# A fused mixer and MoE layer on one core: input rows and router rows transposed by VectorE through DRAM scratch, and the low parts of the mixer's weights kept in DRAM

## The chip, the cores and the metric

The kernel runs on one core of a Trainium2 chip. The metric is the device time of one execution in microseconds (us). Five engines run their own queues in order and meet at semaphores: TensorE (PE; its weight loads are listed as PEld), VectorE (DVE), ScalarE (ACT), GpSimd (POOL) and SyncE (SP), which here only issues DMAs. ScalarE and GpSimd issue DMAs too, and such an instruction, like a wait, holds up whatever stands behind it in its engine's queue.

## The reference

2048 tokens of 1024 channels, all in float32, one layer:

```python
h    = layer_norm(x, ln_in_g, ln_in_b)
proj = h @ w_in                      # (2048, 2048): pool v | gate B | gate C | conv u
pool = (trailing mean over 2/4/8/16 tokens - v) @ pool_w * pool_scale       # 4 groups of 128
conv = gate_b * (causal_depthwise_conv3(gate_c * u) + conv_b)               # 512 channels
h    = layer_norm(ALPHA * h + concat(pool, conv) @ w_out, ln1_g, ln1_b)     # "h1" below
ffn  = MoE(h)    # router h @ w_router (16 experts), softmax, best group of 4, its top 2, silu(x@w1)*(x@w3) @ w2
out  = layer_norm(ALPHA * h + ffn, ln2_g, ln2_b)
```

## The kernel before

**High and low parts.** A float32 product is made of three matmuls in a faster format. Each operand is split into a high part, a copy rounded to that format (ScalarE, `split_hi`), and a low part, the operand less its high part (VectorE, `split_lo`). `three` multiplies high x high, high x low and low x high into one bank of PSUM.

**Chunks and units.** The mixer works through the tokens in 4 chunks of 512 (`NCH`), each of 4 tiles of 128 rows (`TPC`). A chunk has 12 units of weights (`CU`), each 128 x 2048 numbers: units 0 to 7 are columns of `w_in`, two units for each of four groups `g`, and units 8 to 11 are `w_out`. A unit is 48 matmuls. In units 0 to 7 its two halves of 24 are called sections: sections 0 and 1 in the even unit (gate C and u), 2 and 3 in the odd unit (pool v and gate B); section n goes to bank `acc[n]`. Units live in a ring of four slots, `ring_hi` and `ring_lo`. SyncE loads a unit into one of two `stage` buffers, ScalarE makes its high part three units ahead of its use, VectorE its low part. The same 12 units are loaded and split anew in each chunk.

**One unit on the helpers.** All order is written out by hand. For each unit `j` each engine's `chunk` does its share, in this order in its queue. ScalarE: `unit_ahead` (the high part of unit j + 3), then what is listed below for h1, then for an even `j` the high part of the finished convolution and the copy of section 1 to `zext`, for an odd `j` the high part of the pooled product, a convolution tap, the copy of section 2 to `vext`, and the high part of the pooled rows. VectorE: the low part of unit j + 3, then for an even `j` `z_rows` (which reads `zext`) and `conv_lo`, for an odd `j` `pool_mix_lo`, `pool_rows` (which reads `vext`), `conv_rows` and `pooled_split`; after these the normalising `ln_h1` in units 0 to 3, and at the end of an odd unit `gate_rows`.

**The rows of h and h1.** The matmuls need h with channels on the partitions. For chunk c + 1, VectorE normalises the tiles of h in `hrow` during chunk c (`ln_h`), TensorE transposes them 128 x 128 at a time into the banks `tp` (`tr_tile`, before unit 8 and after units 8 to 10), ScalarE and VectorE take high and low parts from there (`tr_hi`, `tr_lo`). GpSimd stores h to DRAM for the residual sum. After a chunk, VectorE adds the residual, and in units 0 to 3 of the next chunk `ln_h1` makes h1 of the four tiles in `hres`; GpSimd stores each (`h1_norm`). In units 2 to 5 TensorE transposes h1 (`h1_tile`), ScalarE copies it to `h1t` (`h1t_copy`, units 3 to 6), TensorE multiplies it by the router's weights (`route_tile`, after units 3 to 6). In units 4 to 7 ScalarE scales h1 by ALPHA and stores it (`alpha_h1`), and in units 5 to 8 it issues the load of the h rows that the residual sum of this chunk needs (`res_load`). The last chunk's h1 goes another way (`h1_last`), and then the experts follow.

## Time and profile before

| | us |
|---|---|
| Median of 3 runs | 1347.22 (1345.38 to 1347.94) |
| The profiled execution | 1347.38 |
| Its span, first to last instruction | 1345.5 |
| TensorE busy | 1310.9 (97%) |
| VectorE busy | 969.2 (72%) |
| ScalarE busy | 510.8 (38%) |
| GpSimd busy | 515.4 (38%) |

The mixer takes the first 600 us, the experts the rest. The page gives the span, the busy time of each engine with its share, and the chain of work that ended last. Views of the trace go closer: windows give one line for each stretch (bounds, length, then busy time and number of instructions of PE, PEld, DVE, ACT and POOL, the granted clock of TensorE as a share of full speed, the busy share of the DMA engines, and GB/s); a timeline gives an engine's instructions by start and duration with the idle time before them and its releaser in brackets. L1194 is line 1194 of the kernel.

### The profile page before, as it was taken

To read this page: it belongs to the slowest core of one execution; us is meant where nothing else is said; L and a number is where in the kernel's file an instruction comes from. 1 tells how busy PE (TensorE), PEld (TensorE's weight loads), DVE (VectorE), ACT (ScalarE), POOL (GpSimd) and SP (SyncE) were. 2 spreads that over 40 slices of the span, in tenths; PEclk is the share of its full clock that TensorE was granted. 3 is DMA by queue.
4 is the path that set the end of the run, shared out by engine and by line. 5 is a ranking of instruction groups with operands and counts; after the bars stand their busy time and mean duration, and the time that the engine had idled before them with its cause. 6 is when DMAs were issued, how large, how long until landed. Compare 5 with 4: busy or idle time off the path is not lost.

```text
span 1345.5 us, 20470 instructions
## 1 busy us (share of the span) xinstructions
PE 1310.9 (97%) x6382; PEld 1096.3 (81%) x6383; DVE 969.2 (72%) x1358; ACT 510.8 (38%) x568; POOL 515.4 (38%) x543
## 2 busy tenths in 40 slices
PE   5999999999999999998999999999999999999995
PEld 5888888888888888887888888888888888888884
DVE  7758577687759786698777885775775677777574
ACT  3423234322343234324444554433442454443351
POOL 2001110111101010022566665656555556665655
PEclk9999999999999999999999999999999999999998
DMA  9625434564455344544877774564555545766421
GB/s 271 177 87 164 147 108 169 163 192 117 156 178 167 111 141 146 208 184 167 307 263 266 264 264 145 190 231 140 183 196 186 184 169 210 237 235 233 152 70 64
DMA packets 156523, 243.59 MB, mean 181 GB/s; under 512 B 18944, under 2 KB 84992, under 8 KB 156480
## 3 DMA queue, kind: packets, MB, share of 16 engines
q1 hardware_dynamic: 118624, 154.15, 35.0%
q0 software_dynamic: 28928, 71.74, 15.1%
q10 hardware_dynamic: 8928, 17.13, 3.7%
q8 instruction: 26, 0.43, 0.1%
q14 instruction: 17, 0.14, 0.0%
HBM read 211.97 MB, written 64.62 MB: 206 GB/s over the span
## 4 chain that ended last, share of the span: by engine, by line
PE 94%; DVE 2%; issue 1%; DMA 1%; POOL 1%; DVEq 0%; ACT 0%; SPq 0%; POOLq 0%
PE acc L520 28%; PE acc L522 28%; PE acc L521 28%; PE tp L560 4%; PE logits L599 2%; PE aux L830 1%; DMA b_in<-in_ln_in_b 1%; PE logits L645 0%; DVE ring_lo L1650 0%; DMA xg<-h_scratch,gat_now 0%; DVE ring_lo L1239 0%; PE aux L522 0%; PE aux L521 0%; PE aux L520 0%; PE aux L670 0%
## 5 line engine op out<-in xcount | busy, mean ns | idle before, releaser
L520 PE MATMUL acc<-ring_hi 128*128 128x512 f32 (+1 forms) x800 | 309.1, 386 | 1.8 <-DVE ring_lo L1239 1.6
L522 PE MATMUL acc<-ring_hi,ring_lo 128*128 128x512 f32 (+1 forms) x800 | 305.7, 382 | 0.0
L521 PE MATMUL acc<-ring_lo,ring_hi 128*128 128x512 f32 (+1 forms) x800 | 305.4, 382 | 0.0
L520 PE MATMUL acc<-ring_hi,xt_hi 128*128 128x512 f32 x648 | 256.4, 396 | 2.4 <-issue 2.2
L522 PE MATMUL acc<-ring_hi,xt_lo 128*128 128x512 f32 x648 | 252.8, 390 | 0.0
L521 PE MATMUL acc<-ring_lo,xt_hi 128*128 128x512 f32 x648 | 252.5, 390 | 0.0
L1803 POOL TENSOR_TENSOR small<-small 128x1 f32<-128x1 f32 x31 | 47.4, 1528 | 360.8 <-DVE small L1208 360.8
L520 PEld LDWEIGHTS acc<-ring_hi 128*128 128x128 f32 x800 | 151.4, 189 | 29.9 <-DVE ring_lo L1239 2.4
L522 PEld LDWEIGHTS acc<-ring_hi,ring_lo 128*128 128x128 f32 x800 | 151.3, 189 | 29.1
L521 PEld LDWEIGHTS acc<-ring_lo,ring_hi 128*128 128x128 f32 x800 | 151.5, 189 | 27.6
L1650 DVE TENSOR_TENSOR ring_lo<-stage_x,ring_hi 128x2048 fp32r<-128x2048 f32 x60 | 161.2, 2727 | 0.2
L921 ACT CAST ring_hi<-stage_x 128x2048 fp32r<-128x2048 f32 x64 | 119.4, 1915 | 77.9 <-PE acc L522 77.3
L520 PEld LDWEIGHTS acc<-ring_hi,xt_hi 128*128 128x128 f32 x648 | 121.9, 188 | 27.2 <-issue 2.8
L522 PEld LDWEIGHTS acc<-ring_hi,xt_lo 128*128 128x128 f32 x648 | 121.6, 188 | 25.6
L521 PEld LDWEIGHTS acc<-ring_lo,xt_hi 128*128 128x128 f32 x648 | 121.8, 188 | 24.0
L916 ACT CAST ring_hi<-stage 128x2048 fp32r<-128x2048 f32 x47 | 89.7, 1909 | 101.5 <-PE acc L522 97.3
L520 PE MATMUL acc<-ring_hi,ht_hi 128*128 128x512 f32 x312 | 125.1, 401 | 0.9 <-DVE ht_lo L1586 0.9
L1194 DVE TENSOR_TENSOR ring_lo<-stage,ring_hi 128x2048 fp32r<-128x2048 f32 x47 | 107.6, 2288 | 20.6 <-ACT ring_hi L916 20.5
L522 PE MATMUL acc<-ring_hi,ht_lo 128*128 128x512 f32 x312 | 121.9, 391 | 0.0
L521 PE MATMUL acc<-ring_lo,ht_hi 128*128 128x512 f32 x312 | 121.6, 390 | 0.0
L1662 DVE TENSOR_TENSOR rrow<-srow,acc 128x512 f32<-128x512 f32 x78 | 49.9, 680 | 95.7 <-PE acc L522 91.8
L1956 POOL DMA_INDIRECT xg<-h_scratch,gat_now x39 | 46.6, 1194 | 146.5 <-PE tp L560 125.9
(277 smaller groups left out, 1922.7 us busy)
## 6 DMA issues: line engine op xcount, KB each, us to landing
stage_x<-in_exp_w SPq DMA_DIRECT2D x64, 1024.0 KB, 6.9
stage<-in_w_in SPq DMA_DIRECT2D x64, 512.0 KB, 5.4
stage<-in_exp_w SPq DMA_DIRECT2D x32, 1024.0 KB, 7.1
stage<-in_w_out SPq DMA_DIRECT2D x32, 512.0 KB, 5.1
h_scratch<-hres POOLq DMA_DIRECT2D x16, 512.0 KB, 3.0
sum_scratch<-hres ACTq DMA_DIRECT2D x16, 512.0 KB, 2.9
hrow<-in_x POOLq DMA_DIRECT2D x12, 512.0 KB, 4.7
h_scratch<-hrow POOLq DMA_DIRECT2D x12, 512.0 KB, 3.0
```

What stands on the lines that cost most here:

```text
L520: nc.tensor.matmul(dst, w_hi, x_hi, start=start, stop=False)
L521: nc.tensor.matmul(dst, w_hi, x_lo, start=False, stop=False)
L522: return nc.tensor.matmul(dst, w_lo, x_hi, start=False, stop=stop)
L560: mm = nc.tensor.transpose(banks[b][:, q, :], rows[:, k * P:(k + 1) * P], ident[:])
L599: mm = nc.tensor.matmul(dst, h1t[:, k, :], wr[:, k, :], start=(k == 0), stop=(k == KT - 1))
L916: nc.scalar.copy(ring_hi[:, slot:slot + 1, :], staged(slot_in)).then_inc(s_hi, 1)
L921: nc.scalar.copy(ring_hi[:, j:j + 1, :], staged(j)).then_inc(s_ehi[j // 2], 1)
L1194: V.tensor_tensor(lo, staged(slot_in), hi.bitcast(F32), ALU.subtract).then_inc(s_lo, 1)
L1650: V.tensor_tensor(ring_lo[:, j:j + 1, :], staged(j), ring_hi[:, j:j + 1, :].bitcast(F32), ALU.subtract).then_inc(s_elo[w], 1)
L1662: ins = V.tensor_tensor(rrow[:, cols], srow[:, cols], acc[2 + n][:], ALU.add)
L1803: G.tensor_tensor(rstd[:], vareps[:], half[:], ALU.pow).then_inc(s_rstd, 1)
L1956: G.indirect_dma_start(xg[:], None, h1_dram, bass.IndirectOffsetOnAxis(ap=index[:, 0:1], axis=0), bounds_check=SEQ - 1, oob_is_err=False). ...
```

## The change

The changed kernel does three things otherwise.

**VectorE transposes.** VectorE's transpose works within blocks of 32 x 32. So that these blocks are enough, a tile is first rearranged in quarters through DRAM: for h, GpSimd stores the normalised tile in that arrangement (`h0_rows`) and loads it back (`h_back`), VectorE transposes it into the banks `tp` (`h_turn`); for h1, ScalarE loads the stored h1 rows back into `hres` with four DMAs of 32 partitions (`h1_back`), and VectorE transposes them straight to `h1t` (`h1_turn`). The channels come out in another order (`(p k)` in place of `(k p)`), so `w_in` and `w_router` are loaded in that order, and the transposes that stay on TensorE (chunk 0 and the last h1) read with a step of eight numbers. `tr_tile` for chunks 1 to 3, `h1_tile` and `h1t_copy` are gone.

**Places.** `alpha_h1` moves from units 4 to 7 to units 1 to 4, `h1_back` stands in units 2 to 5, `res_load` in units 4 to 7 with a wait for `h1_turn`; `h1_turn` stands at the end of VectorE's units 3 to 6; `route_tile` stands in the middle of TensorE's units 4 to 7. `ln_h` of tile 1 moves from unit 7 to unit 6.

**Low parts.** Only the 12 low parts of chunk 0 are computed. SyncE stores them to DRAM (`keep_lo`), and for the other 36 units it loads them back (`back_lo`), each 1 MB, two units behind the load of the unit itself. TensorE waits for the high part and for that load (`unit_split`).

```diff
+            def keep_lo(u):
+                sp.dma_start(lo_dram[u], ring_lo[:, u % RING1, :].bitcast(F32)).then_inc(s_kept[u % RING1], 16)
+            def back_lo(u):
+                if u < CU + RING1:
+                    sp.wait_ge(s_kept[u % RING1], 16 * (CU // RING1))
+                sp.dma_start(ring_lo[:, u % RING1, :].bitcast(F32), lo_dram[u % CU]).then_inc(s_back[u % RING1], 16)
...
+            for u in range(CU, MU):
+                if u < CU + 2:
...
+                else:
+                    sp.wait_ge(s_hi, u - 1)
+                    load_mixer(u % CU)
+                    back_lo(u - 2)
...
+            def unit_split(u):
+                if u < CU:
+                    pe.wait_ge(s_lo, u + 1)
+                else:
+                    pe.wait_ge(s_hi, u + 1)
+                    pe.wait_ge(s_back[u % RING1], 16 * ((u - CU) // RING1 + 1))
...
             def route_tile(c, t):
-                pe.wait_ge(s_h1tc, (c * TPC + t + 1) * 2)
+                pe.wait_ge(s_h1turn, c * TPC + t + 1)
...
                         section(slot, which, sct).then_inc(s_sec[sct], 1)
+                        if not first and which == 0 and j >= 4:
+                            route_tile(c - 1, j - 4)
...
-                    if not first:
-                        if 3 <= j < 7:
-                            route_tile(c - 1, j - 3)
-                        if 2 <= j < 6:
-                            h1_tile(c - 1, j - 2)
...
             def alpha_h1(c, t):
                 act.wait_ge(s_h1out[t], c * 16 + 16)
-                act.wait_ge(s_h1t, (c * TPC + t + 1) * 2)
+                if c == NCH - 1:
+                    act.wait_ge(s_h1t, (t + 1) * 2)
...
+            def h1_back(c, t):
+                act.wait_ge(s_ahout[t], c * 16 + 16)
+                rows = h1_dram[(c * TPC + t) * P:(c * TPC + t + 1) * P, 0:D].rearrange("(r b) (a f) -> a r b f", r=SUB, a=QUARTERS)
+                for a in range(QUARTERS):
+                    dst = hres[a * SUB:(a + 1) * SUB, t, :].rearrange("r (b f) -> r b f", b=QUARTERS)
+                    act.dma_start(dst, rows[a]).then_inc(s_h1q[t], 16)
...
-                    if not first and 3 <= j < 7:
-                        h1t_copy(c - 1, j - 3)
+                    if not first and 1 <= j < 5:
+                        alpha_h1(c - 1, j - 1)
+                    if not first and 2 <= j < 6:
+                        h1_back(c - 1, j - 2)
                     if not first and 4 <= j < 8:
-                        alpha_h1(c - 1, j - 4)
-                    if not first and 5 <= j < 9:
-                        res_load(c, j - 5)
+                        res_load(c, j - 4)
...
             def unit_ahead(c, j, last):
                 ja = j + RING1 - 1
-                if ja >= CU and last:
+                if c * CU + ja >= CU:
                     return
...
+            def h_turn(c, t):
+                dve.wait_ge(s_xq[t % 2], ((c - 1) * 2 + t // 2 + 1) * 16)
+                dve.wait_ge(s_trlo, (c * TPC + t) * 2)
+                by_k = hrow[:, t % 2, :].rearrange("p (b c k) -> p k b c", b=QUARTERS, c=SUB)
+                for h in range(2):
+                    V.transpose(tp[h][:].rearrange("p q (r b) -> p q b r", r=SUB), by_k[:, 4 * h:4 * h + 4]).then_inc(s_tr, 1)
+            def h1_turn(c, t):
+                dve.wait_ge(s_h1q[t], (c + 1) * 16 * QUARTERS)
+                dve.wait_ge(s_log, c * TPC + t)
+                if c >= 1 and t == 0:
+                    dve.wait_ge(s_lst, c)
+                V.transpose(h1t[:].rearrange("p k (r b) -> p k b r", r=SUB),
+                            hres[:, t, :].rearrange("p (b c k) -> p k b c", b=QUARTERS, c=SUB)).then_inc(s_h1turn, 1)
...
+                    if not first and 3 <= j < 7:
+                        h1_turn(c - 1, j - 3)
                     if not last:
-                        if j in (5, 7):
-                            ln_h(c + 1, (j - 5) // 2, nth())
+                        if j in (5, 6):
+                            ln_h(c + 1, j - 5, nth())
+                        if j == 7:
+                            h_turn(c + 1, 0)
```

On ScalarE, in units 1 and 2 of chunk 2, the queue of before reads (L1023 is the convolution tap, L916 the high part of a coming unit, L1028 the copy to `vext`, L955 the high part of a convolution, L1016 the copy to `zext`):

```order
L1023 ACTIVATE cacc<-zext,cb,cw 128x512 [waits mix_lo,z_ready]
L1028 COPY vext<-acc 128x512 [waits pooled,sec_v]
L1030 CAST ring_hi<-sum_a 128x512 [waits pooled]
L916 CAST ring_hi<-stage 128x2048 [waits stage1_in,sec_b]
L955 CAST ring_hi<-cacc 128x512 [waits conv_rows]
L1016 COPY zext<-acc 128x512 [waits sec_u,conv_rows]
```

and that of the changed kernel, where the same steps have lines L1061, L951, L1066, L990 and L1054:

```order
L1001 ACTIVATE hres<-hres 128x1024 [waits h1_out0]
L1003 DMA sum_scratch<-hres 128x1024 [waits alpha_h1]
L1061 ACTIVATE cacc<-zext,cb,cw 128x512 [waits mix_lo,z_ready]
L1066 COPY vext<-acc 128x512 [waits pooled,sec_v]
L1068 CAST ring_hi<-sum_a 128x512 [waits pooled]
L951 CAST ring_hi<-stage 128x2048 [waits stage1_in,sec_b]
L1001 ACTIVATE hres<-hres 128x1024 [waits h1_out1]
L1003 DMA sum_scratch<-hres 128x1024 [waits alpha_h1]
L1011 DMA hres<-h_scratch 32x4x256 [waits alpha_h1_out0]
L1011 DMA hres<-h_scratch 32x4x256 x3
L990 CAST ring_hi<-cacc 128x512 [waits conv_rows]
L1054 COPY zext<-acc 128x512 [waits sec_u,conv_rows]
```

The scaling (L1001), its store (L1003) and the loads of h1 rows (L1011) stand ahead of the tap, of the copy to `vext` and of the copy to `zext`; before, they came from unit 4 on.

On VectorE, at the end of unit 3 and the start of unit 4 of chunk 2, before (L1287 is `pooled_split`, L1216 the last step of normalising the fourth tile of h1, L1292 `gate_rows`, L1194 a unit's low part, L1246 the start of `z_rows`):

```order
L1287 TENSOR_TENSOR ring_lo<-sum_a,ring_hi 128x512 [waits pooled_hi_done,dve_chain]
L1204 BN_STATS small<-hres 128x6 [waits res_taken]
L1205 BN_STATS small<-hres 128x6
L1207 BN_AGGR small<-small 128x2 [waits dve_chain]
L1208 TENSOR_SCALAR small<-small 128x1 [waits dve_chain]
L1212 SCALAR_TENSOR_TENSOR hres<-hres,small,g_52 128x1024
L1216 SCALAR_TENSOR_TENSOR hres<-hres,small,b_53 128x1024 [waits rstd_ready,dve_chain]
L1292 TENSOR_TENSOR cacc<-cacc,acc 128x512 [waits sec_b]
L1194 TENSOR_TENSOR ring_lo<-stage,ring_hi 128x2048 [waits unit_hi]
L1246 COPY zext<-zhist 128x2 [waits sec_u_free,sec_c]
```

and in the changed kernel:

```order
L1344 TENSOR_TENSOR ring_lo<-sum_a,ring_hi 128x512 [waits pooled_hi_done,dve_chain]
L1244 BN_STATS small<-hres 128x6 [waits res_taken]
L1245 BN_STATS small<-hres 128x6
L1247 BN_AGGR small<-small 128x2 [waits dve_chain]
L1248 TENSOR_SCALAR small<-small 128x1 [waits dve_chain]
L1252 SCALAR_TENSOR_TENSOR hres<-hres,small,g_52 128x1024
L1256 SCALAR_TENSOR_TENSOR hres<-hres,small,b_53 128x1024 [waits rstd_ready,dve_chain]
L1349 TENSOR_TENSOR cacc<-cacc,acc 128x512 [waits sec_b]
L1288 STREAM_TRANSPOSE h1t<-hres 128x8x4x32 [waits lists_done,logits_done,h1_quarters_in0]
L1303 COPY zext<-zhist 128x2 [waits sec_u_free,sec_c]
```

The low part is gone, and the transpose of the first tile of h1 (L1288) stands behind the normalising of the fourth.

On TensorE, the router product of the first tile of h1 in chunk 2 (L599 before) stood between units 3 and 4, beside the transposes of the second tile (L560):

```order
L521 MATMUL acc<-ring_lo,ring_hi 128x512
L522 MATMUL acc<-ring_hi,ring_lo 128x512
L599 MATMUL logits<-wr,h1t 128x16 [waits h1_t_copied]
L599 MATMUL logits<-wr,h1t 128x16 x7
L560 MATMUL tp<-ident,hres 128x128 [waits h1_t_copied,h1_rows]
L560 MATMUL tp<-ident,hres 128x128 x7
L520 MATMUL acc<-ring_hi 128x512 [waits sec_c_free,unit_lo]
L521 MATMUL acc<-ring_lo,ring_hi 128x512
```

In the changed kernel (L639) it stands between the two sections of unit 4 and waits for VectorE's transpose:

```order
L556 MATMUL acc<-ring_hi 128x512
L557 MATMUL acc<-ring_lo,ring_hi 128x512
L558 MATMUL acc<-ring_hi,ring_lo 128x512
L639 MATMUL logits<-wr,h1t 128x16 [waits h1_quarters_turned]
L639 MATMUL logits<-wr,h1t 128x16 x7
L556 MATMUL acc<-ring_hi 128x512 [waits sec_u_free]
L557 MATMUL acc<-ring_lo,ring_hi 128x512
```

## Rows read from the trace of the kernel before

**Rows 1.** The page: the span, and busy time of the engines

```profile
span 1345.5 us, 20470 instructions
...
PE 1310.9 (97%) x6382; PEld 1096.3 (81%) x6383; DVE 969.2 (72%) x1358; ACT 510.8 (38%) x568; POOL 515.4 (38%) x543
```

**Rows 2.** Windows, chunks 1 and 2: busy us, clock, DMA share, GB/s

```profile
160.00:309.00 149.00, 149.00 (x728) 125.18 (x727) 107.22 (x167) 50.34 (x58) 19.74 (x21) 1.00 0.50 156
309.00:457.00 148.00, 148.00 (x728) 124.16 (x727) 111.82 (x194) 48.49 (x58) 18.67 (x19) 1.00 0.48 150
```

**Rows 3.** Chain that ended last, chunk 2: start us, us, what

```profile
318.77 0.89 PE aux L670 x8
...
342.15 0.87 PE tp L560 x8
...
353.95 1.69 PE logits L599 x16
355.64 0.92 PE tp L560 x8
...
408.63 0.88 PE tp L560 x8
```

**Rows 4.** Timeline of VectorE, end of chunk 1 and chunk 2: start, us, instruction

```profile
291.81 1.28 DVE L1216 SCALAR_TENSOR_TENSOR hrow<-hrow,small,b_in 128x1024 f32<-128x1024 f32 x1 [0.54 <-POOL small L1803]
...
323.97 1.28 DVE L1216 SCALAR_TENSOR_TENSOR hres<-hres,small,b 128x1024 f32<-128x1024 f32 x1 [0.54 <-POOL small L1803]
...
327.98 0.17 DVE L1259 COPY vext<-vhist 128x16 f32<-128x16 f32 x1
...
336.94 0.68 DVE L1292 TENSOR_TENSOR cacc<-cacc,acc 128x512 f32<-128x512 f32 x1
...
351.32 0.16 DVE L1259 COPY vext<-vhist 128x16 f32<-128x16 f32 x1
...
355.65 0.69 DVE L1287 TENSOR_TENSOR ring_lo<-sum_a,ring_hi 128x512 fp32r<-128x512 f32 x1
...
361.01 0.68 DVE L1292 TENSOR_TENSOR cacc<-cacc,acc 128x512 f32<-128x512 f32 x1
361.61 2.28 DVE L1194 TENSOR_TENSOR ring_lo<-stage,ring_hi 128x2048 fp32r<-128x2048 f32 x1
```

**Rows 5.** Timeline of ScalarE, chunk 2, the same columns

```profile
325.18 0.59 ACT L1028 COPY vext<-acc 128x512 f32<-128x512 f32 x1 [3.21 <-PE acc L522]
...
371.33 1.08 ACT L973 ACTIVATE hres<-hres 128x1024 f32<-128x1024 f32 x1
372.44 0.33 ACTq L975 DMA_DIRECT2D sum_scratch<-hres  x1
372.86 0.39 ACTq L981 DMA_DIRECT2D hres<-h_scratch  x1
```

**Rows 6.** Timeline of GpSimd, the store of chunk 1's first h1 rows

```profile
325.85 0.58 POOL L1830 DMA_DIRECT2D h_scratch<-hres  x1 [1.99 <-DVE hres L1216]
```

**Rows 7.** Stores of h1 rows (line L1830), issue to landing

```profile
DMA to landing us min/median/max: 2.9/3.0/4.0
```

**Rows 8.** Stores of scaled h1 rows (line L975), issue to landing

```profile
DMA to landing us min/median/max: 2.6/3.0/5.5
```

**Rows 9.** DMA issues of one line: KB each, median us to landing

```profile
hres<-h_scratch ACTq DMA_DIRECT2D x12, 512.0 KB, 4.8
```

**Rows 10.** Timeline of VectorE, two reductions of the same 256 elements

```profile
422.54 0.42 DVE L1323 TENSOR_REDUCE lost<-wins 128x64 f32<-128x256 f32 x1
422.88 0.60 DVE L1323 TENSOR_REDUCE won<-wins 128x64 f32<-128x256 f32 x1
```

**Rows 11.** Timeline of TensorE at the start, matmuls with 256 columns

```profile
17.66 0.58 PE L520 MATMUL acc<-ring_hi 128*128 128x256 f32 x1 [1.63 <-DVE ring_lo L1239]
...
21.67 0.34 PE L520 MATMUL acc<-ring_hi 128*128 128x256 f32 x1
...
24.35 0.28 PE L521 MATMUL acc<-ring_lo,ring_hi 128*128 128x256 f32 x1
```

More of the change, by code:

```diff
@@ L64 @@
 ROW = D + NE
+SUB = 32
+QUARTERS = P // SUB
 ALIGN = 128
@@ L97, in build, with h0_tile, h0_rows @@
     h0_dram = nc.dram_tensor("h0_scratch", (SEQ, D), F32).ap()
+    def h0_tile(tile):
+        return h0_dram[tile * P:(tile + 1) * P, :]
+    def h0_rows(tile):
+        return h0_tile(tile).rearrange("(a r) (b f) -> (r b) a f", r=SUB, b=QUARTERS)
     h1_dram = nc.dram_tensor("h1_scratch", (SEQ, ROW), F32).ap()
@@ L352, in build @@
         s_lo = sem("unit_lo")
+        s_kept = [sem(f"slot{i}_lo_stored") for i in range(RING1)]
+        s_back = [sem(f"slot{i}_lo_loaded") for i in range(RING1)]
         s_used = sem("unit_used")
@@ L384, in build @@
         s_h1t = sem("h1_transposed")
+        s_h1q = [sem(f"h1_quarters_in{t}") for t in range(TPC)]
+        s_h1turn = sem("h1_quarters_turned")
         s_h1tc = sem("h1_t_copied")
@@ L486, in _ @@
                     x_first(j + 2)
-            for c in range(1, NCH):
-                for j in range(CU):
-                    sp.wait_ge(s_lo, c * CU + j - 1)
-                    load_mixer(j)
+                else:
+                    keep_lo(j - 2)
+            for u in range(CU, MU):
+                if u < CU + 2:
+                    sp.wait_ge(s_lo, u - 1)
+                    load_mixer(u % CU)
+                    keep_lo(u - 2)
+                else:
+                    sp.wait_ge(s_hi, u - 1)
+                    load_mixer(u % CU)
+                    back_lo(u - 2)
+            for u in range(MU, MU + 2):
+                sp.wait_ge(s_hi, u - 1)
+                back_lo(u - 2)
             def load_expert(ex, j):
@@ L553, in first_units, with transpose_h @@
                             elif bank == 2:
-                                tr_tile(0, 2)
+                                tr_tile(2)
+            def transpose_h(rows, banks):
+                by_k = rows.rearrange("p (c k) -> p k c", k=KT)
+                for b in range(2):
+                    for q in range(4):
+                        mm = nc.tensor.transpose(banks[b][:, q, :], by_k[:, 4 * b + q, :], ident[:])
+                    mm.then_inc(s_tr, 1)
             def transpose_tile(rows, sem_out, banks=tp):
@@ L713, in chunk @@
                     if j == 8:
-                        if not last:
-                            tr_tile(c + 1, 0)
                         pe.wait_ge(s_mix, (c * NG + 3) * 2)
@@ L735, in chunk @@
                         list_tiles(c - 1)
-                    if not last and j < CU - 1:
-                        tr_tile(c + 1, j - 7)
                 if last:
-                    pe.wait_ge(s_lo, c * CU + CU)
+                    unit_split(c * CU + CU - 2)
+                    unit_split(c * CU + CU - 1)
                     for t in range(TPC):
@@ L959, in route_exp @@
                 nc.scalar.activation(rt[c].prob[:], rt[c].shift[:], ACT.Exp).then_inc(s_exd, 1)
-            def h1t_copy(c, t):
-                if c >= 1 and t == 0:
-                    act.wait_ge(s_lst, c)
-                for b in range(2):
-                    act.wait_ge(s_h1t, (c * TPC + t) * 2 + b + 1)
-                    nc.scalar.copy(h1t[:, 4 * b:4 * b + 4, :], tp[b][:]).then_inc(s_h1tc, 1)
             def alpha_h1(c, t):
                 act.wait_ge(s_h1out[t], c * 16 + 16)
-                act.wait_ge(s_h1t, (c * TPC + t + 1) * 2)
+                if c == NCH - 1:
+                    act.wait_ge(s_h1t, (t + 1) * 2)
                 nc.scalar.mul(hres[:, t, :], hres[:, t, :], ALPHA).then_inc(s_ah, 1)
@@ L1504, in chunk @@
                         if j == 11:
+                            residual(c, 1, 0)
+                            h_turn(c + 1, 3)
+                            residual(c, 1, 1)
                             tr_lo(c + 1, 3)
-                            for t in range(TPC):
-                                residual(c, 1, t)
+                            residual(c, 1, 2)
+                            residual(c, 1, 3)
                     else:
```

63 lines of the change are left out of this document (37 added, 26 removed).

## Prediction

> **What bounds the kernel now.** I read the page first: TensorE is busy for 1310.9 of a span of 1345.5 us, VectorE for 969.2 [rows 1]. A busy TensorE could still be waiting on something, so I took the stretches by chunk next: in chunks 1 and 2 TensorE is busy for every microsecond at the full granted clock, while VectorE has 107 to 112 us of work in some 149 and the DMA engines are half used [rows 2]. So in the mixer every instruction taken off TensorE is worth its whole time, as long as nothing starts to make TensorE wait. The chain that ended last shows what such an instruction costs [rows 3]: eight transposes of one tile take 0.87 to 0.92 us, and a unit of 48 matmuls takes 353.95 - (342.15 + 0.87) = 10.93 us, so half a unit (one section) 5.47. After the matmuls I read the three helpers in chunk 2, because the change rewires them: VectorE [rows 4], ScalarE [rows 5] and GpSimd's stores [rows 6 to 8].
>
> **The change, part by part.**
>
> *Transposes off TensorE.* 12 tiles of h and 12 of h1, eight transposes each. The rows give 0.88 for a tile of h, 0.87 for the first tile of h1 in a chunk, and 0.92 for the other three, which follow a router product [rows 3]: 12 x 0.87 + 12 x 0.91 = **-21.3 us**, all of it on the chain.
>
> *VectorE's load.* 36 subtractions of 2048 elements go, 2.28 us each [rows 4]: -82 us. 24 block transposes of 512 elements and 12 of 1024 come. No row of before has one. The nearest is a pair of reductions over the same 256 elements: read in order 0.42 us, read with a step of 16 bytes 0.60 us [rows 10]. That is 0.7 ns more for each element. VectorE does 2048 elements in 2.28 us and 512 in 0.69 us [rows 4], so 1.04 ns an element and a fixed 0.16; with the step 0.16 + 512 x 1.74 ns = 1.05 us, and 1.94 us for 1024. Bounds: 0.69 and 1.22 us if the step costs nothing, and 3 us and 6 us if each element takes three such steps. I take 1.05 and 1.94, together 48 us: VectorE's load falls by 34 us. The Trainium skill, "Vector Engine (DVE) Microarchitecture Reference", on the reshape front-end, says that the transposing array sustains one element per cycle per lane; by that the two would be 0.69 and 1.22 us. The sum would fall by 3 x 0.7 = 2 us, since only one h1 transpose per chunk lies on the path below.
>
> *The low parts.* They are read back right after the high part of the same unit is made, three units (33 us) before TensorE wants them, and 1 MB more on the queue is hidden by that. Traffic of a chunk grows from 150 GB/s x 148 us = 22 MB [rows 2] by 12.6 MB of low parts and 4.2 MB of rows read back, so the share of the DMA engines goes from 0.48 to some 0.8. Cost nothing by themselves; without that cover a unit would wait for its load.
>
> *The round trip of h.* Tile 3 of h is the last: before, its normalising ended at 293.1 [rows 4] and the next chunk began at 318.77 - 10.93 = 307.8 [rows 3], 14.7 us. After, there are 0.6 + 3.0 us of store, some 4.8 of load (what the residual rows take [rows 9]), 2.1 of transposes, and 1.9 for its high and low parts: 12.4 us. It fits with 1 to 2 us to spare. Nothing charged.
>
> *The wait that the change adds.* This is the term that decides. The scaling of h1 on ScalarE (`alpha_h1`) moves from units 4 to 7 to units 1 to 4. It waits for the store of the normalised row, and VectorE normalises tile t only in unit t. Behind the scaling, ScalarE's queue holds the copy of the section that VectorE's next step reads (`vext`, `zext`). So each tile now goes VectorE, store, ScalarE, VectorE, with nothing beside it, and TensorE waits at the end, at the router product of tile 0, which now stands in the middle of unit 4. I walk chunk 2 on the clock of the trace of before:
> - Tile 0: rows ready at 325.25 [rows 4], store issued 325.85 [rows 6], landed 3.0 later [rows 7] at 328.9. ScalarE scales and issues in 1.11 + 0.42 = 1.53 us [rows 5], 330.4. Then a convolution tap of some 0.75 and the `vext` copy of 0.59 [rows 5]: 331.7. Before, that copy was done at 325.8 [rows 5].
> - VectorE from the pooling of unit 1 to the end of normalising tile 1 needs 336.94 - 327.98 = 8.96 us [rows 4]: 340.7. Store issued 341.3, landed 344.3, scaled and issued 345.9, four `h1_back` issues of 0.42 [rows 5]: 347.5, two more ScalarE steps of 512 elements (high part, `zext` copy), 1.1: 348.6.
> - VectorE: 1.5 us for z and a low part (two steps of 512 elements and small ones), 4.75 to normalise tile 2 (361.01 - 355.65 less 0.61 [rows 4]): 354.9. Store landed 358.5, scaled 360.0, issues 361.7, pooled high part, tap, `vext`: 363.6.
> - VectorE, pooling of unit 3 to the end of tile 3: 361.01 - 351.32 = 9.69 us [rows 4]: 373.3. Gate 0.6, `h1_turn` 1.94: 375.8.
> - TensorE: unit 3 starts at 342.15 as before but without the transposes, ends at 353.1, first section of unit 4 at 358.5. It waits for tile 0's transposed rows until 375.8: **17.3 us**.
>
> Nothing later in the chunk waits by the same walk: the transposes of tiles 1 to 3 come a unit apart and VectorE is ahead again by unit 7. Three chunks: **+52 us**.
>
> *What the loaded queues add.* Three stores of each chunk lie in that walk, nine in all, and each comes while up to 2 MB for a coming unit is under way. Measured stores land in 2.6 to 5.5 us [rows 7, 8]. I charge 0.5 us over the median: **+4.5** (bounds 0 and 9 x 2 = 18). The Trainium skill, "DMA: Bandwidth & Descriptors", section "Issuing engines are not separate DMA queues", says that the queues of all issuing engines run on the same 16 DMA engines and interleave, which speaks for the upper bound, by which the sum would be 14 us more.
>
> *TensorE's clock.* The only long idle time of before is at the start, and after it matmuls of 256 columns came every (21.67 - 17.66) / 19 = 0.211 us, later every (24.35 - 21.67) / 22 = 0.122 [rows 11]: the rates of 1.2 and 2.4 GHz. The 19 slow ones cost 19 x 0.089 = 1.7 us. Three waits of 17 us: **+5.2**. The Trainium skill, "TensorE: Matmul & The Clock Gate", section "Why this matters for your kernels", warns of idle gaps between bursts of matmuls for this reason; by it the term stands, without it the sum is 5 us less.
>
> *Strided transposes that stay.* 64 transposes on TensorE (chunk 0 and the last h1) now read with a step of 32 bytes. No row shows it. If the step costs TensorE what it costs VectorE, two thirds more on 128 reads of 0.42 ns, that is 0.036 us each: **+2.3** (bounds 0 and 7).
>
> **Sum**, against the profiled execution's own 1347.38 us (span 1345.5; the median of three runs is 1347.22): -21.3 + 52 + 4.5 + 5.2 + 2.3 = +42.7, so **1390 us**, 3.2% slower.
>
> **The rivals.**
> - *The stores do not hold the chain* (another side). If ScalarE's wait is covered, VectorE reaches the pooling of unit 3 at about 348.3 and `h1_turn` ends 9.69 + 0.6 + 1.94 later, at 360.5: a wait of 2 us a chunk, too short for the clock. 1347.4 - 21.3 + 6 + 2.3 = 1334 us. It decides if ScalarE passes the first scaling by about 326. Against it: VectorE finishes tile 0 only at 325.25, and no store landed in under 2.6 us. Even stores of 0 us would leave 17.3 - 9 = 8 us of wait by the walk. 0.10.
> - *Transposes by VectorE are far dearer.* At 3 and 6 us one h1 transpose lies on the chain (+4 a chunk), 6 x 2 us of h transposes break the slack of tile 3, and 24 us a chunk leave VectorE near its limit: +30 to +55 on the forecast, 1420 to 1445. At 2 and 4 us, 1403. 0.10.
> - *Crowded DMA.* Stores of 5 us and h tile 3 late by 2 us: 1390 + 13.5 + 6 = 1410. The share of 0.8 speaks for it; against it, no h1 store of before took over 4.0 us [rows 7]. 0.10.
> - *A part of the chain is shorter than walked*, for instance tile 3's normalising starts earlier: waits of 8 to 12 us, 1365 to 1375. 0.08.
>
> **How the numbers follow.** Forecast 0.62, with its own range of 1376 to 1405 (the bounds of the store and clock terms). A difference within 0.2% can't be told from none here. Faster is the first rival and a little of the last, 0.10; same 0.02; slower 0.88. For the range I leave out the first rival and the dear end of the second: 1364 to 1418.
>
> **What would show it.** Right: in the profile after, TensorE waits once in each of chunks 1 to 3, in unit 4, before the router product, for VectorE's transpose, 15 to 20 us each; ScalarE's scaling of h1 waits 3 to 8 us for a DMA; a chunk takes about 160 us instead of 149; matmuls after the wait come at half rate for some microseconds. No wait stands before a unit for its low part. Wrong: TensorE's waits in the mixer are short, or they stand elsewhere (start of a chunk: the round trip of h; start of a unit: the low parts), or a block transpose takes over 2 us.

## The result and the profile after

The changed kernel takes 1436.3 us (median of 4 runs, 1432.7 to 1437.1) against 1346.5 us for the kernel before on the same chip: ratio 1.066, 95% interval 1.065 to 1.068. It is 89.8 us slower; the forecast was 43 slower. One run of scale_later below, at a granted clock of 0.75 in place of 0.98, took 1648.4 us and is left out of its median.

The page of the changed kernel, span and busy times, to be held against [rows 1]:

```profile
span 1434.5 us, 20188 instructions
...
PE 1315.8 (92%) x6190; PEld 1093.1 (76%) x6191; DVE 938.3 (65%) x1358; ACT 500.2 (35%) x544; POOL 519.3 (36%) x555
```

TensorE has 192 instructions fewer and VectorE 31 us less work, yet the span is 89 us longer. TensorE's idle time grew by 84.1 us and its busy time by 4.9, although some 21 us of transposes are gone: a first sign that other matmuls got slower. Two windows of the mixer, about one chunk each (columns as in [rows 2]; from one first router product to the next it is now 175.7 and 183.2 us, where it was 148.8):

```profile
160.00:345.00 185.00, 158.37 (x710) 130.67 (x709) 101.80 (x195) 46.90 (x52) 21.87 (x25) 0.92 0.70 233
345.00:512.00 167.00, 135.63 (x609) 112.22 (x607) 95.30 (x164) 43.67 (x48) 20.93 (x23) 0.91 0.67 221
```

Three things differ from [rows 2]: TensorE stands still for 27 and 31 us, its granted clock is 0.92 and 0.91 in place of 1.00, and the DMA engines are 0.7 busy in place of 0.5. The list of TensorE's waits says what it waits for (engine, output and line; then us in total, times, longest):

```profile
PE logits L639 <- DVE h1t L1288: 66.9, 3, 22.6
PE tp L605 <- DVE hres L1256: 11.6, 1, 11.6
PE acc L556 <- DVE zhist L1306: 11.1, 3, 3.9
PE acc L556 <- DVE ring_lo L1296: 7.4, 2, 5.7
```

L1288 is `h1_turn`: the router product of tile 0 waits 22 us in the middle of unit 4, once in each of chunks 1 to 3. L1306 is the end of `z_rows`: the start of unit 4 waits 3.3 to 3.9 us, again in each. L1296 is the low part of an input tile: one wait of 5.7 us at the start of chunk 3. (The 11.6 us stand at the kernel's start, before as after.) ScalarE in chunk 2 shows where this comes from; its timeline:

```profile
344.10 0.59 ACT L1054 COPY zext<-acc 128x512 f32<-128x512 f32 x1 [9.03 <-PE acc L558]
...
357.89 1.06 ACT L1001 ACTIVATE hres<-hres 128x1024 f32<-128x1024 f32 x1 [11.39 <-DMA h_scratch<-hres]
358.98 0.34 ACTq L1003 DMA_DIRECT2D sum_scratch<-hres  x1
...
360.15 0.57 ACT L1066 COPY vext<-acc 128x512 f32<-128x512 f32 x1
...
375.59 1.06 ACT L1001 ACTIVATE hres<-hres 128x1024 f32<-128x1024 f32 x1 [10.19 <-DMA h_scratch<-hres]
376.68 0.34 ACTq L1003 DMA_DIRECT2D sum_scratch<-hres  x1
377.06 2.61 ACTq L1011 DMA_DIRECT2D hres<-h_scratch  x4
...
380.24 0.58 ACT L1054 COPY zext<-acc 128x512 f32<-128x512 f32 x1
```

Each scaling (L1001) waits 10 to 11 us until the store of its rows has landed, and the copies that VectorE reads (L1066, L1054) come right behind it. The chain that ended last runs through exactly these, and gives the length of a store on it (start, us, what):

```profile
368.56 1.29 DVE hres L1256
369.90 0.54 issue
370.44 5.13 DMA h_scratch<-hres
375.59 1.07 ACT hres L1001
...
387.78 5.54 DMA h_scratch<-hres
393.34 1.06 ACT hres L1001
...
409.73 1.98 DVE h1t L1288
411.75 3.60 PE logits L639 x16
415.35 0.61 PE acc L556
415.96 0.43 PE acc L557
```

So the forecast's mechanism is there, step by step, but a store takes 5.1 and 5.5 us here where 3.0 to 3.5 were charged, and the first router product takes 3.6 us in place of 1.69 [rows 3]. Matmuls behind it come every 0.43 us (1.2 GHz), later every 0.23 (2.4 GHz).

### The profile page after: what moved, and what is told of

It is laid out like the page before. It is cut to its first block, busy times and chain, and to the rows that moved or that the text cites. A ratio compares the mean times of both kernels' runs of the same rounds, so it can differ in the third digit from the quotient of the medians.

```text
span 1434.5 us, 20188 instructions
## 1 busy us (share of the span) xinstructions
PE 1315.8 (92%) x6190; PEld 1093.1 (76%) x6191; DVE 938.3 (65%) x1358; ACT 500.2 (35%) x544; POOL 519.3 (36%) x555
## 4 chain that ended last, share of the span: by engine, by line
PE 72%; DVE 11%; DMA 7%; issue 4%; POOL 2%; ACT 2%; ACTq 1%; SPq 0%; DVEq 0%; POOLq 0%
PE acc L556 22%; PE acc L558 22%; PE acc L557 22%; DMA h_scratch<-hres 3%; PE tp L612 2%; POOL small L1869 2%; PE logits L639 2%; DMA h_scratch<-hrow 1%; PE aux L865 1%; DMA hrow<-in_x 1%; DMA hrow<-h_scratch 1%; ACTq L1011 1%; DVE hres L1256 1%; DVE tp L1280 1%; DVE small L1244 1%
## 5 line engine op out<-in xcount | busy, mean ns | idle before, releaser
L556 PE MATMUL acc<-ring_hi 128*128 128x512 f32 (+1 forms) x800 | 315.7, 395 | 19.4 <-DVE zhist L1306 11.1
L557 PE MATMUL acc<-ring_lo,ring_hi 128*128 128x512 f32 (+1 forms) x800 | 311.7, 390 | 0.0
L558 PE MATMUL acc<-ring_hi,ring_lo 128*128 128x512 f32 (+1 forms) x800 | 311.6, 389 | 0.0
L556 PEld LDWEIGHTS acc<-ring_hi 128*128 128x128 f32 x800 | 155.9, 195 | 52.1 <-issue 19.2
L558 PEld LDWEIGHTS acc<-ring_hi,ring_lo 128*128 128x128 f32 x800 | 155.3, 194 | 30.8
L557 PEld LDWEIGHTS acc<-ring_lo,ring_hi 128*128 128x128 f32 x800 | 155.8, 195 | 29.3
L1869 POOL TENSOR_TENSOR small<-small 128x1 f32<-128x1 f32 x31 | 44.7, 1443 | 351.3 <-DVE small L1248 351.2
L951 ACT CAST ring_hi<-stage 128x2048 fp32r<-128x2048 f32 x47 | 89.8, 1910 | 58.3 <-PE acc L558 49.5
L2007 POOL TENSOR_TENSOR orow<-arow,b 128x1024 f32<-128x1024 f32 x39 | 93.3, 2393 | 1.1 <-ACT arow L1158 1.1
```

The source lines that it names most:

```text
L556: nc.tensor.matmul(dst, w_hi, x_hi, start=start, stop=False)
L557: nc.tensor.matmul(dst, w_hi, x_lo, start=False, stop=False)
L558: return nc.tensor.matmul(dst, w_lo, x_hi, start=False, stop=stop)
L951: nc.scalar.copy(ring_hi[:, slot:slot + 1, :], staged(slot_in)).then_inc(s_hi, 1)
L1869: G.tensor_tensor(rstd[:], vareps[:], half[:], ALU.pow).then_inc(s_rstd, 1)
L2007: G.tensor_tensor(orow[:], arow[:], b_2[:], ALU.add).then_inc(s_fo, 1)
```

## Experiments

All ratios are to the kernel before on the same chip, with the 95% interval.

### Where the chain is held

**scale_later**: only ScalarE's order is changed: the scaling, the loads behind it and the residual loads each come one unit later.

```diff
-                    if not first and 1 <= j < 5:
-                        alpha_h1(c - 1, j - 1)
-                    if not first and 2 <= j < 6:
-                        h1_back(c - 1, j - 2)
-                    if not first and 4 <= j < 8:
-                        res_load(c, j - 4)
+                    if not first and 2 <= j < 6:
+                        alpha_h1(c - 1, j - 2)
+                    if not first and 3 <= j < 7:
+                        h1_back(c - 1, j - 3)
+                    if not first and 5 <= j < 9:
+                        res_load(c, j - 5)
```

> Edit: in the changed kernel ScalarE scales each router tile (alpha_h1) one unit later (units 2 to 5), and h1_back and res_load follow one unit later. If the chain goes through ScalarE's scaling, which waits for the store of rows that were normalised in the unit before, the three waits of the router product (66.9 us), the three of zext's order (11.1 us) and their slow matmuls (about 19 us) nearly all go, and the wait for the input tile 3 (5.7 us with 2.8 us of slow matmuls) stays: 1436 less 90 to 97 gives 1339 to 1346 us, at most 1355. If VectorE's own order and the place of the router product in the middle of unit 4 set the wait, h1_turn still ends after it and less than a third goes: above 1400. If the crowded transfers set it, it falls in part: 1365 to 1400, with single waits at loads in many places.

Measured: 1370.5 us (1.016, 1.014 to 1.018). 66 us came back. ScalarE's waits for these stores fell from 125.2 us (12 times) to 3.6 (6 times), though the median store of h1 rows now lands only after 7.0 us. TensorE's waits:

```profile
PE logits L639 <- DVE h1t L1288: 14.7, 4, 5.4
PE acc L556 <- DVE ring_lo L1296: 13.8, 4, 6.1
```

The expectation missed by 15 us at its near end, because two things stay: 4 to 5 us before each router product, and the trip of input tile 3, now late three times (by 0.7, 6.1 and 5.3 us).

**turn_first**: VectorE does `h1_turn` ahead of `ln_h1`.

> Edit: in the changed kernel VectorE does h1_turn of a unit ahead of ln_h1, in place of behind it, and nothing else. If ScalarE's chain of stores sets the wait, the quarters of tile 0 come too late anyway and VectorE now stands at the turn with ln_h1(3) behind it: 1433 to 1450 us. If VectorE's order sets the wait (the turn stands behind ln_h1(3), 4 us), the three waits of 22 us lose about 4 to 6 us each: 1415 to 1424.

Measured: 1426.6 us (1.059, 1.054 to 1.063), between the two expectations. VectorE's order is worth some 10 of 90 us (runs of 1418.6 to 1431.8 against 1432.7 to 1437.1); the first waits for L1288 in each chunk were still 15 to 20 us.

**route_end**, and **later_route_end** (the same on top of scale_later): the product leaves the middle of the unit.

```diff
-                        if not first and which == 0 and j >= 4:
-                            route_tile(c - 1, j - 4)
...
                     if j % 2 == 0 and g > 0:
                         pool_map(c, g - 1)
+                    if not first and j >= 4:
+                        route_tile(c - 1, j - 4)
```

> Edit: the changed kernel with the router products at the end of units 4 to 7 in place of the middle, nothing else. If h1_turn of tile 0 comes at a time that TensorE does not set, each of three waits gets shorter by what now lies ahead of it (half a unit and the pool map, 5.5 + 0.7 = 6.2 us) and the slow clock stays: 1436.3 - 19 = 1414 to 1420 us. If the chain has a step that waits for the section behind the product (VectorE's gate or z of unit 4), the wait moves there and little is won: 1428 to 1437.

> Edit: as scale_later, and the router product of a tile stands at the end of units 4 to 7, behind both sections and the pool map, in place of the middle. In scale_later the wait for h1_turn was 4 to 5 us before each first product; 12 matmul groups of half a unit (7 us) now lie ahead of it, so these waits (14.7 us), the slow first products (about 5.7 us) and about 4 us of slow matmuls go: 1346 to 1352 us. If VectorE's turns only end later, because they wait for something that TensorE does in between, the waits stay and it is 1365 to 1375.

Measured: route_end 1422.2 us (1.056, 1.055 to 1.058), 14 us better than the changed kernel and not the 16 to 22 of the first expectation. Its waits:

```profile
PE aux L556 <- DVE ring_lo L1344: 29.7, 3, 13.0
PE logits L639 <- DVE h1t L1288: 17.0, 3, 5.7
```

L1344 is the pooled split, which the pool map ahead of the product reads. It hangs on the same late chain, so part of the wait only moves forward to it. later_route_end took 1342.8 us (0.996, 0.994 to 0.997; six runs, 1336.5 to 1348.4): 28 us less than scale_later, 3 less than expected, and 0.4% faster than the kernel before. So with the scaling one unit later VectorE is only 5 us too late for the middle of unit 4, and the end of the unit covers it.

### The parts of the change one at a time

**lo_made** leaves out the stored and reloaded low parts (VectorE splits every unit again), **low_only** puts that part alone into the kernel before.

> Edit: the changed kernel without the part on the low parts: VectorE makes them in every chunk as in the kernel before, and nothing is stored or reloaded; both turns through scratch stay. If the chain of stores sets the wait and its stores take 5.0 us in place of 3.0 because of the reloads, each of three chunks gets three times 2 us back, 18 us, less what 36 more splits of VectorE put into the chain: 1410 to 1430 us. If the crowded transfers are the main cause, most of the loss goes: below 1380. If VectorE is what the chain lacks, it gets slower: above 1445.

> Edit: the kernel before with the part on the low parts alone: stored in the first chunk, reloaded behind it, all transposes on TensorE as before. In this kernel no store is waited for in the middle of the mixer with less than several us to spare, so the theory of the chain expects no change: 1343 to 1350 us, whatever the transfers take. If the reloads by themselves hold TensorE up (low parts that land late), it is slower by several us: 1355 to 1400, with waits at the matmuls for slot loads.

Measured: lo_made 1414.7 us (1.050, 1.049 to 1.052), low_only 1346.8 (1.000, 0.999 to 1.001). In low_only the median store of h1 rows takes 5.2 us, as in the changed kernel, and nothing waits for it; in lo_made it takes 2.9. The mean busy share of the DMA engines from 200 to 500 us is 0.49 before, 0.70 in low_only and 0.53 in lo_made. The changed kernel's row of these issues (queue, number, size, median us to landing):

```profile
h_scratch<-hres POOLq DMA_DIRECT2D x16, 512.0 KB, 5.1
```

The same row of lo_made:

```profile
h_scratch<-hres POOLq DMA_DIRECT2D x16, 512.0 KB, 2.9
```

And of low_only:

```profile
h_scratch<-hres POOLq DMA_DIRECT2D x16, 512.0 KB, 5.2
```

So the reloads cost nothing alone and 21.6 us beside the trips through scratch. TensorE's three waits for `h1_turn` in lo_made are still 21 to 22 us; what is gone are the wait at the start of unit 4 and that for input tile 3, with their slow matmuls, and TensorE is that much earlier at the product. VectorE's splits are back, but they are not on this chain: they run while ScalarE waits for the store (chunk 2 of lo_made; L1208 is the split, L977 the scaling, L987 `h1_back`):

```profile
364.32 2.28 DVE L1208 TENSOR_TENSOR ring_lo<-stage,ring_hi 128x2048 fp32r<-128x2048 f32 x1
367.37 1.06 ACT L977 ACTIVATE hres<-hres 128x1024 f32<-128x1024 f32 x1 [8.00 <-DMA h_scratch<-hres]
368.84 3.41 ACTq L987 DMA_DIRECT2D hres<-h_scratch  x4
```

From the first rows ready (347.56) to the end of `h1_turn` (402.33) the chain of lo_made takes 54.8 us.

**router_only** and **input_only** take back the trip of the other rows; TensorE transposes those again.

> Edit: the changed kernel with the input rows turned on TensorE again (from strided rows, without the trip through scratch); the router rows still go through scratch and VectorE, low parts reloaded. If the chain through the router rows' stores carries the loss, only the wait of tile 3 (5.7 us and 2.8 us of slow matmuls) goes and 48 groups of transposes of 0.88 us for 10.6 us come back: 1434 to 1443 us. If the queues of the input rows (24 more large transfers, 12 of them waited for on GpSimd) are what makes it slow, it falls below 1420.

> Edit: the changed kernel with the router rows turned on TensorE again as in the kernel before (h1_tile, h1t_copy, scaling in units 4 to 7); the input rows still go through scratch and VectorE, low parts reloaded. If the router rows carry the loss: 1346.8 less 10.6 us of transposes, plus the wait of tile 3 with its slow matmuls (8.5 us as in the changed kernel, 19 us as in scale_later): 1344 to 1356 us. If the input rows' trip or the crowded queues carry it: above 1380.

Measured: router_only 1437.8 us (1.067, 1.066 to 1.069), input_only 1344.2 (0.998, 0.997 to 0.999). The loss belongs to the router rows' part (their trip, the place of the scaling and the place of the product, which input_only takes back together). The input rows' trip with the reloads loses nothing: it gives 3 of the 10.6 us of its transposes.

### The hold without the trip

**hold_scalar** adds one wait to the kernel before; **hold_scalar_low** adds the reloads to that.

```diff
+                    if not first and 1 <= j < 5:
+                        act.wait_ge(s_h1out[j - 1], (c - 1) * 16 + 16)
                     if not first and 3 <= j < 7:
                         h1t_copy(c - 1, j - 3)
```

> Edit: the kernel before with one wait more on ScalarE in units 1 to 4 of chunks 1 to 3: for the store of the router rows that VectorE normalised in the unit before (h1_out), where the changed kernel has it; no transpose, transfer or instruction is changed. If this hold is what stretches the chain, TensorE waits in units 3 and 4 of each chunk, 10 to 25 us each: 1375 to 1425 us. If the hold costs nothing by itself and the trip through scratch and VectorE's turn behind it are needed for a wait, it stays at 1346 to 1352.

> Edit: the kernel before with both the hold on ScalarE (hold_scalar, 1366 us by itself) and the stored and reloaded low parts (low_only, 1347 us by itself, stores of router rows at 5.2 us in place of 3). If the reloads cost time because they stretch stores that a chain waits for, the two together cost more than their sum of 19 us: nine stores of 2 us more, less 36 splits that VectorE no longer has in that chain; 1372 to 1385 us. If the stretched stores are hidden, or the missing splits win as much: 1355 to 1368.

Measured: hold_scalar 1366.3 us (1.014, 1.013 to 1.016), between its two expectations (1346 to 1352, 1375 to 1425); hold_scalar_low 1385.1 (1.028, 1.026 to 1.029), at the upper end of its range. One wait instruction in each of four units a chunk costs 19 us though no other work is changed; the rest of the 90 comes with the trip, the turn behind it and the product's new place. The reloads cost 0 us in the kernel before and 19 us in the one that holds ScalarE: the median store of router rows goes from 3.0 to 4.6 us, and ScalarE's waits for them, 12 in each kernel, from 98.0 us in all to 120.4. TensorE's wait in hold_scalar:

```profile
PE logits L599 <- ACT h1t L967: 8.5, 4, 3.6
```

The same in hold_scalar_low:

```profile
PE logits L631 <- ACT h1t L1000: 24.1, 4, 8.7
```

### What the idle time does to the clock

**filled_wait**: matmuls of no use to the result stand in the wait.

```diff
                         if not first and which == 0 and j >= 4:
+                            if j == 4:
+                                for i in range(100):
+                                    nc.tensor.matmul(tp[0][:].rearrange("p q r -> p (q r)"),
+                                                     ht_v[0][:, i % KT, 0:P], ring_hi[:, slot, i % 4 * 512:i % 4 * 512 + 512],
+                                                     start=True, stop=True)
                             route_tile(c - 1, j - 4)
```

> Edit: the changed kernel with 100 matmuls of 512 columns, of no use to the result, in front of the first router product in unit 4 of chunks 1 to 3, into a PSUM bank that is free there: they fill 21.5 to 22 us in which TensorE waited. If the slow first product (3.6 in place of 1.7 us) and the slow matmuls behind it come from the idle time, each of three chunks gets 4 to 5 us back: 1420 to 1426 us. If matmuls are slow behind any such wait, or in this part for another reason, it stays at 1433 to 1445.

Measured: 1416.0 us (1.054, 1.051 to 1.057), 20.3 us less than the changed kernel, with more work in it, and 4 us under the expectation. Behind the fill the product takes 1.85 us and the matmuls come every 0.23 us at once:

```profile
231.80 5.15 PE L734 MATMUL tp<-ring_hi 128*128 128x512 f32 x22
236.79 1.85 PE L639 MATMUL logits<-wr,h1t 128*128 128x16 f32 x16
238.49 0.49 PE L556 MATMUL acc<-ring_hi 128*128 128x512 f32 x1
238.82 0.40 PE L557 MATMUL acc<-ring_lo,ring_hi 128*128 128x512 f32 x1
239.05 0.40 PE L558 MATMUL acc<-ring_hi,ring_lo 128*128 128x512 f32 x1
```

In the changed kernel the slow products and matmuls behind the three long waits make 13 us by its trace, and they are gone here. In the profiled run the trip of input tile 3 also was in time (5.7 us and 2.8 us of slow matmuls), which is about the rest.

### Toward a better version

**later_end_h3** starts tile 3's trip earlier, **tile3_tensor** gives that tile back to TensorE; both on top of later_route_end.

> Edit: as later_route_end, and VectorE normalises input tile 3 (ln_h) in unit 9, behind tr_lo of tile 1, in place of unit 10 behind four residuals. If the waits at the start of a chunk (0.7, 6.1 and 5.3 us in scale_later) are the trip of tile 3 through scratch, which begins with that ln_h, they go too, with some 5.5 to 7 us of slow matmuls: 1328 to 1337 us, faster than the kernel before by about 1 per cent. If these waits are for the low parts of the last tile behind VectorE's residuals, and not for the trip, nothing changes against later_route_end: 1346 to 1352.

> Edit: as later_route_end, and input tile 3 of each chunk is turned by TensorE in unit 10 from its strided rows, without the trip through scratch; the other three go through scratch. If the waits at the start of a chunk (12 us) and their slow matmuls (5.8 us) are this trip, they go and 3 x 1.76 us of transposes come back: 1342.8 less 12.5 gives 1326 to 1334 us, about 1.2 per cent faster than the kernel before. If another tile's trip takes its place, 1340 to 1348.

Measured: later_end_h3 1355.1 us (1.006, 1.005 to 1.007), worse than without the edit and outside both expectations. TensorE now waits for residuals:

```profile
PE acc L556 <- DVE hres L1371: 19.0, 3, 8.3
```

VectorE's timeline in that kernel says why:

```profile
286.05 1.27 DVE L1252 SCALAR_TENSOR_TENSOR hrow<-hrow,small,g_in 128x1024 f32<-128x1024 f32 x1
290.77 1.28 DVE L1256 SCALAR_TENSOR_TENSOR hrow<-hrow,small,b_in 128x1024 f32<-128x1024 f32 x1 [3.45 <-POOL small L1869]
291.98 1.28 DVE L1371 SCALAR_TENSOR_TENSOR hres<-hres,acc 128x512 f32<-128x512 f32 x2
```

The inverse root of tile 3 (L1869) stands on GpSimd behind `h_back` of tile 2, which waits 4.95 us for that tile's store. VectorE stands for it, and the residuals stand behind VectorE. tile3_tensor took 1340.2 us (0.995, 0.994 to 0.996), as its second expectation has it: the tile 3 waits are gone, but tile 2's trip is late once by 5.4 us in chunk 0, and 5.3 us of transposes are back.

**route_end_lo_made** (later_route_end without the reloads), **later_lo_made** (scale_later without them) and **tile3_lo_made** (tile3_tensor without them):

> Edit: as later_route_end, with the low parts made by VectorE in every chunk and no reloads. If the trip of tile 3 is late because the reloads stretch its store and its load, it is in time without them and up to 18 us go: 1326 to 1335 us. If VectorE's splits then stand in the way of the trip, it stays at 1338 to 1350.

> Edit: scaling one unit later, and low parts made by VectorE in every chunk, no reloads. Against scale_later (1372 us) the trip of tile 3 has stores of 3 us in place of 5 to 7, so the 12 us at the chunk starts and their 5.8 us of slow matmuls shrink to some 6 us, and the waits for h1_turn in unit 4 (4 to 5 us) stay or grow by VectorE's split: 1355 to 1366 us. If VectorE's splits cost more than the reloads did: above 1372.

> Edit: route_end_lo_made with input tile 3 of each chunk turned by TensorE in unit 10 (no trip through scratch). It takes away the two waits of 2.9 us that route_end_lo_made has left in unit 0 with 1.7 us of slow matmuls and adds 3 x 1.76 us of transposes: 1333 to 1338 us, the same as route_end_lo_made within its interval. If another wait stood behind those: 1339 to 1345.

Measured: route_end_lo_made 1337.2 us (0.993, 0.992 to 0.995), between its two expectations and the fastest version, though its interval touches that of tile3_tensor: both turns on VectorE, scaling one unit later, products at the end, low parts made by VectorE. later_lo_made 1366.9 (1.015, 1.013 to 1.016), 1 us over its range; its three waits for L1262 (`h1_turn`) are 5.25, 5.25 and 5.28 us, since VectorE's own order ends that late. tile3_lo_made 1342.5 (0.996, 0.995 to 0.998), not the 1333 to 1338 that was expected but its alternative: the two waits of 3 us are still there. They are not tile 3's trip but unit 10's residuals, behind VectorE's split and normalising.

## Why the prediction was wrong

The direction and the mechanism were right: the wait is at the router product in the middle of unit 4, once a chunk, for `h1_turn`, and ScalarE's scaling behind a store makes it (scale_later takes 66 of 90 us back by moving that alone). The time was outside the range. By the forecast's own steps, in us:

| Step | forecast | measured |
|---|---|---|
| Transposes taken off TensorE | -21.3 | not seen singly; 192 instructions gone |
| "The wait that the change adds" and "What the loaded queues add" | +52 +4.5 | 66.9 + 11.1 = +78.0 |
| "TensorE's clock" | +5.2 | +21.9 |
| "The round trip of h" | 0 | +5.7 |
| "Strided transposes that stay" | +2.3 | about +1 |
| Low parts by themselves | 0 | 0 (low_only) |
| Sum | +42.7 | about +85 of 89.0 in the span |

The waits of the table make 83.7 of the 84.1 us of idle time that TensorE gained; the 4 us that are not placed are in its busy time.

**The step that failed first is "What the loaded queues add".** It charged 0.5 us a store over 3.0, 4.5 us in all, and gave 18 as its upper bound; the stores on the chain took 8.4 us a chunk more than 3.0 each, some 25 in all if chunk 2 stands for the three. In chunk 2, from the first rows ready (350.51) to the end of `h1_turn` (411.71), the chain takes 61.2 us; the walk had 325.25 to 375.8, 50.6. The difference by parts: the three stores 6.8, 5.1 and 5.5 in place of 3.0 each, +8.4, and two groups of four `h1_back` issues 2.6 in place of 1.7, +1.8.

These issues are a term of the walk itself ("The wait that the change adds"), and without the reloads they are dearer still: 3.4 and 3.2 us in lo_made, whose chain of 54.8 us is 4.2 over the walk with stores of 3.7, 3.0 and 3.0 us on it. So part of the miss, the three waits of 21 to 22 us against 17.3, doesn't need slow stores. The 10.6 us a chunk are not all wait, since TensorE itself now comes later to the product by its wait at the start of unit 4 and the slow matmuls behind it. VectorE's stretches on the chain were right within 0.2 us each (9.1 against 8.96, 6.4 against 6.3, 12.4 against 12.2).

The store rows read for the price [rows 7, 8] were of a kernel whose DMA engines were half busy; the change raises that share to 0.7 by its own reloads, and hold_scalar_low shows what that does: 19 us, where stores are waited for. The mean share alone doesn't set the price. SyncE issues a reload (median 8.6 us to landing) 3 to 4 us before each of the three stores of chunk 2, for instance before that at 370.44:

```profile
366.72 0.99 SPq L505 DMA_DIRECT2D ring_lo<-lo_scratch  x1
```

The scaled rows' stores (L1003), as large and at the same mean share, are issued there 10 to 11 us behind a reload, and landed in 3.0 us (median), as before. The rival "Crowded DMA" had this mechanism and its 5 us at a chance of 0.10; it said 1410, and most of what is left is the clock. The Trainium skill's rule in "DMA: Bandwidth & Descriptors", section "Issuing engines are not separate DMA queues", that all queues share the same 16 DMA engines, given in the prediction beside the upper bound, agrees with this: the reloads are issued by SyncE, the stores that got longer by GpSimd.

Of the 26 us of waits a chunk, 3.3 to 3.9 come at the start of unit 4, where the forecast saw no wait: the bank of section 0 comes free only behind `z_rows` of unit 2, which is on the late chain. In lo_made that wait is absent.

**The second is "TensorE's clock", mis-sized by a factor of four.** It charged 19 slow matmuls behind each long wait, at the 0.089 us that one of 256 columns loses, and took a wait of 2 us to be free. The matmuls here have 512 columns and lose 0.2 each. Measured: 7.5 us of slow matmuls behind the three long waits (10 to 14 matmuls each), 5.9 us behind the three short ones, 2.8 behind tile 3's, and 3 x 1.9 for the router product itself, whose 16 small matmuls are the first behind the wait. filled_wait takes 13 us of it back. The warning of the Trainium skill, "TensorE: Matmul & The Clock Gate", section "Why this matters for your kernels", about idle gaps between bursts agrees with this trace. That a wait of 3.8 us already halves the rate shows in the timeline of the changed kernel:

```profile
382.02 0.77 PE L556 MATMUL acc<-ring_hi 128*128 128x512 f32 x1 [3.77 <-DVE zhist L1306]
382.59 0.63 PE L557 MATMUL acc<-ring_lo,ring_hi 128*128 128x512 f32 x1
383.01 0.63 PE L558 MATMUL acc<-ring_hi,ring_lo 128*128 128x512 f32 x1
...
385.45 0.39 PE L558 MATMUL acc<-ring_hi,ring_lo 128*128 128x512 f32 x1
```

**"The round trip of h"** left 1 to 2 us to spare with a store of 3.0 and a load of 4.8. The slack is gone in one chunk of three, in scale_later in all three. In the late one (ahead of chunk 3) both transfers took far more than charged (rows of the chain that ended last: start, us, what):

```profile
491.01 9.05 DMA h_scratch<-hrow
...
500.62 7.86 DMA hrow<-h_scratch
```

Longer medians alone don't do it: in the changed kernel they are 5.7 and 4.8, in input_only 6.3 and 7.1, and there TensorE does not wait for tile 3 at all.

**Right:** the block transposes are nearly as cheap as taken, though those of h1 are over the 2 us that the forecast named as a sign of being wrong; the row groups (first one h1 tile, then half an h tile; us in all, then mean ns) are 2.2 and 1.15 us against 1.94 and 1.05, and well over the lower bounds of 1.22 and 0.69:

```profile
L1288 DVE STREAM_TRANSPOSE h1t<-hres 128x1024 f32<-128x1024 f32 x12 | 26.6, 2215 | 0.0
L1280 DVE STREAM_TRANSPOSE tp<-hrow 128x512 f32<-128x512 f32 x24 | 26.4, 1147 | 21.7 <-DMA hrow<-h_scratch 21.7
```

The low parts cost and gain nothing by themselves, VectorE is not the bound, and the rival by which the stores do not hold the chain is out. Of the signs of being right, the place and cause of the long waits came, but each size is larger: 21.9 to 22.6 us in place of 15 to 20, ScalarE's waits 10 to 11 in place of 3 to 8, a chunk 176 in place of 160. The strided transposes of the last h1 tiles take at most 0.34 us each against 0.31, and eight of chunk 0 take 0.90 against 0.87.

## What to carry to other kernels

A wait for a transfer on an engine whose queue also feeds the critical path can hold everything behind it: 98 us of such waits on ScalarE cost 19 us in hold_scalar, and taking away nearly all of the 125 us in the changed kernel gave 66 back. Ask what stands behind the wait, and try the instruction one unit later. Price the transfers of such a chain at the load that the change itself brings, and by what is under way when they are issued, not at the load of the old profile, and ask of each extra transfer not what it costs but who waits for its neighbours: the same reloads cost 0 us in one order and 19 to 22 in another. Add to each long stall of TensorE its restart at half rate, including the small matmuls that come first.

## What was not expected of the hardware

- Short waits can halve TensorE's rate too. Behind the waits of 3.3 to 3.9 us in the changed kernel matmuls of 512 columns came every 0.43 us, the rate of 1.2 GHz, in place of 0.23, that of 2.4 GHz. One wait of 2.4 us was followed by the same (start of a chunk in route_end), another of 2.4 us was not (filled_wait), nor was one of 3.2 us (chunk 3 of route_end). The runs don't say what decides.
- GpSimd's stores of h1 rows, 512 KB each, landed in 2.9 us (median) with the DMA engines half busy (0.53, lo_made) and in 4.6 (hold_scalar_low, 0.65) to 7.0 (scale_later, 0.75) with the reloads. ScalarE's stores of the same size took 3.0 in the changed kernel (0.70).
- ScalarE needed 0.65 us for each of the `h1_back` issues (2.61 for four; 3.2 and 3.4 in lo_made), 0.34 for a whole-tile store.
- TensorE transposes rows read with a step of 32 bytes at nearly the price of plain ones (0.90 us against 0.87 for eight).
